# Every fifth weight tile of one phase fetched as 120 and 8 partitions

## The chip, the core and the metric

The kernel runs on one core of a Trainium2 chip. The core has five engines with a queue of instructions each: TensorE (PE, with its weight loads as PEld), VectorE (DVE), ScalarE (ACT), GpSimd (POOL) and SyncE (SP). Transfers between main memory and the on-chip memory, whose rows are 128 partitions, run on 16 DMA engines, whichever queue asks for them. The metric is the device time of one execution, in microseconds.

## What is computed

Two transformer blocks over 256 tokens of width 1024, in 32-bit floats. The first block (two attentions, gates, a mixture of 32 experts) and the even layer of the second lie before the change. The phase around the change is the second block's two PEER layers, with the odd layer's short-convolution mixer between them:

```python
def short_conv_mixer(xn, w_in, conv_w, w_out):
    bg, cg, hx = jnp.split(xn @ w_in, 3, axis=-1)
    u = cg * hx
    y = conv(u, conv_w)            # 3 taps along the tokens, causal
    return (bg * y) @ w_out

def peer(xn, w_q, sub_keys, u, v):
    q = (t @ w_q).reshape(n_tok, 8, 2, 128)
    # two top-16 lists per head, top 16 of their sums: eidx; softmax: gate
    hid = gelu(einsum('td,thkd->thk', t, u[eidx]), approximate=False)
    return einsum('thk,thkd->td', gate * hid, v[eidx])
```

Each token of each PEER layer picks 8 x 16 rows of two tables of 16,384 rows. A final norm follows.

## The kernel before, in words

The tokens are two chunks of 128, one token per partition. The PEER work is a list of 512 positions, `SLOTS`: layer, chunk, head, and which of the head's 16 picks. For each position GpSimd asks for one gather (`pool_ask`, L2812): 128 rows, one per token, of 8 KB each (the row of u and the row of v side by side), 1 MiB in all, into one of nine row buffers. VectorE multiplies the u half with the tokens and sums (L2714), ScalarE applies gelu and the gate (L2768, L2771) and makes a diagonal matrix of the result (L2777), and TensorE multiplies that with the v half and adds into two banks (L2700). Some positions take the last step on VectorE instead (L2720). GpSimd runs five positions ahead (`AHEAD`), and a gather into a buffer waits until the position that used the buffer before is finished. Each gather raises its buffer's semaphore by 16, and VectorE waits for that.

All other work of the phase is laid beside the positions by a table written out by hand (`beside`): at a position p each engine does its part of what `put` placed there. The odd mixer's input products (`"in"`, TensorE L2407), its output products (`"out"`, L2432), the second layer's queries (`"q"`, L2450) and the choosing of the picks on VectorE (L2566 to L2680) are laid out so.

The weights of these products come as tiles of 128 partitions x 8 KB, 1 MiB. SP loads them in `sync_peer` (L2291) in the order of the table with `load` (L270, its DMA is L275). `rings.next_slot` names the slot; SP waits until TensorE has done with the tile that was there, and issues one DMA which raises the slot's semaphore by 16. There are six ring slots and one more tile in the arena; from the middle of the first chunk on only three slots rotate, and four tiles of the mixer and five of the queries serve both chunks. TensorE waits in `tile` for the value that the semaphore has after the tile of that name. The three kinds are 20, 8 and 11 loads, 39 in all.

Of the kernel before, what the change touches and what calls it, by code (L numbers as in the profile page):

```python
# [96 lines left out]
def build(nc, a, out):  # L97
    ctx = ExitStack()
    with ctx:
# [5 lines left out]
        def signal(name):  # L105
            signals.append(Signal(ctx.enter_context(nc.semaphore(name))))
            return signals[-1]

        def table(missing):
            tables.append(Table(missing))  # L110
            return tables[-1]

        pe, ve, ac, po = signal("s_pe_done"), signal("s_dve_done"), signal("s_act_done"), signal("s_pool_done")
        landed = [signal(f"s_slot_landed{i}") for i in range(NSLOT + NX)]
# [7 lines left out]
        slot_of, spent = table(0), table((pe.sem, 1))  # L122
# [74 lines left out]
        rings = Rings()  # L197
# [72 lines left out]
        def load(e, name, src, place=None):  # L270

            s, before = rings.next_slot(name, place)
            if before is not None:
                e.wait_ge(*spent[before])
            e.dma_start(place_of(s)[:, 0:src.shape[1]], src).then_inc(landed[s].sem, landed[s].up(name, by=16))  # L275

        def place_of(s):

            if s < NSLOT:
                return ring[:, s, :]  # L280
            return kept_tile if s == NSLOT else arena[:, 2048 * (s - NSLOT):2048 * (s - NSLOT + 1)]
# [14 lines left out]
        def load_tiles(e, name, w, at_, c0, n, kn=8):  # L296
            for i, (k, m) in enumerate(parts(n, kn)):
                load(e, (name, c0, k), w[at_ + i])
# [140 lines left out]
        def sp_residual(e, n, w):  # L439
            for c0 in (0, 512):  # L440
                for k in (0, 4):
                    load(e, ("res" + n, c0, k), w[c0 // 256 + k // 4])
# [240 lines left out]
        def causal_part(c, lhsT, rhs_of):  # L683
            return (lhsT, rhs_of(0, (c + 1) * P), (c + 1) * P, cm[:, 0:P] if c == 0 else cm[:, P:384], 1.0)
# [21 lines left out]
        def sp_fill_step(e, c0, half):  # L706
            if c0 >= 5664 and half == 0:
                lo = c0 - 5664
                load(e, ("bias", c0), row(b_gate[lo:lo + 512], 512))
            load(e, ("in", c0, 4 * half), w_in[IN_AT[c0] + half])  # L710
# [24 lines left out]
        for c in range(2):  # L735
            for h in range(8):
                mla_jobs.append(dict(
                    c=c, parts=[causal_part(c, qT[:, h, c * P:(c + 1) * P], lambda lo, hi, h=h: kT[:, h, lo:hi])],
# [6 lines left out]
                    c=c, parts=[(qd[p0:p0 + 64, 4 * g + h // 2, c * P:(c + 1) * P],  # L745
                                 kd[p0:p0 + 64, 4 * g + h // 2, 0:kw], kw,
                                 Bm[:, bo + g * kw:bo + (g + 1) * kw], -8.0 * slope) for g in range(3)],
# [1028 lines left out]
        def join_tile(c, c0, k):  # L1776
            return ("join again", c0, k) if c else ("join", c0, k)
# [403 lines left out]
        w_q, w_odd, w_odd_out = a["c_w_q"], a["c_odd_w_in"], a["c_odd_w_out"]  # L2181
# [21 lines left out]
        KEPT_Q = {3: 4, 4: 5, 5: NSLOT, 6: 3, 7: None}  # L2203

        def odd_tile(c, j, k):
            part = (*OB[c][j], k)
            return ("odd", "both", *part) if part in KEPT else ("odd", c, j, k)

        def q_tile(c, h):
            return ("wq", 1, "both", h) if h in KEPT_Q else ("wq", 1, c, h)  # L2210
        OCOL = {"bg": 0, "cg": 1024, "hx": 2048}
# [6 lines left out]
        def norm_steps(p, n, c):  # L2218
            put(p, "square", n, c)
            put(p + 1, "mean", n, c)  # L2220
            put(p + 2, "normed", n, c)
# [66 lines left out]
        put(2 * SEG + 20, "gain", "fin", "mix1")  # L2288
        norm_steps(3 * SEG + 4, "fin", 0)

        def sync_peer(e):  # L2291
            load(e, ("wq", 0, 2), w_q[0, 2], 0)
            load(e, ("wq", 0, 3), w_q[0, 3], 1)
            load(e, ("wq", 0, 4), w_q[0, 4], 2)
            load(e, join_tile(1, 0, 0), w_e_out[0], 3)
            load(e, ("wq", 0, 5), w_q[0, 5], 4)
            load(e, join_tile(1, 0, 4), w_e_out[1], 5)
            load(e, join_tile(1, 512, 0), w_e_out[2], 3)
            load(e, join_tile(1, 512, 4), w_e_out[3], 5)
            load(e, ("wq", 0, 6), w_q[0, 6], 3)  # L2300
            load(e, ("wq", 0, 7), w_q[0, 7], 5)
            for h in range(2):
                load(e, ("wq again", h), w_q[0, h], 5)
            e.wait_ge(ve.sem, ve.at(("joined", 1, 512)))
            for p in range(LAST):
                for what in beside.get(p, ()):
                    if what[0] == "in" and what[3] % 4 == 0:
                        _, c, j, k = what
                        part, hf = OB[c][j]
                        kept = KEPT.get((part, hf, k))  # L2310
                        if kept is None or c == 0:
                            if kept == NSLOT:
                                rings.narrow(3)
                            load(e, odd_tile(c, j, k), w_odd[(OCOL[part] + 512 * hf) // 256 + k // 4], kept)
                    if what[0] == "out" and what[3] % 4 == 0:
                        _, c, hf, k = what
                        load(e, ("oddout", c, hf, k), w_odd_out[2 * hf + k // 4])
                    if what[0] == "q" and what[3] == 0:
                        _, c, h, _ = what
                        if c == 0 or h not in KEPT_Q:  # L2320
                            load(e, q_tile(c, h), w_q[1, h], KEPT_Q.get(h))

        def pe_score(e, L, h, cs_):
            lo, hi = P * cs_[0], P * (cs_[-1] + 1)
# [518 lines left out]
        def sync(e):  # L2843
            sync_first(e)
            sync_moe(e)
            sync_even(e)
            sync_peer(e)
            e.wait_ge(ve.sem, ve.at(("xn", "fin", 0)))
            g = fetched("out0")
            e.dma_start(out[0, 0:P, :], xn[:, 0, :]).then_inc(g.sem, g.up("all", by=16))  # L2850
            g = fetched("out1")
            for c0 in (0, 512):
                e.wait_ge(ve.sem, ve.at(("xn", "fin", 1, c0)))
                e.dma_start(out[0, P:2 * P, c0:c0 + 512], xn[:, 1, c0:c0 + 512]).then_inc(g.sem, g.up("all", by=16))
            for c in range(2):
                g = fetched(f"out{c}")
                e.wait_ge(g.sem, g.at("all"))
# [142 lines left out]
```

## Time and profile before

| | |
|---|---|
| median of 3 runs | 2153.95 us (2153.48 to 2160.74) |
| the profiled execution | 2157.04 us, span 2155.2 us |
| granted TensorE clock, mean | 0.967 of full speed |
| PE / DVE / ACT / POOL busy | 86% / 60% / 33% / 31% |
| software-made DMA queue (gathers) | 542.37 MB, 61.0% of 16 engines |
| SP's DMA queue (weights) | 227.75 MB, 26.3% |

The profile is one execution. "Idle before" in a group is the time in which an engine had nothing running before such an instruction, with what ended it. The chain is followed back from the last instruction to what released each step. DMA share is the mean busy share of the 16 DMA engines, so that one engine of 16 alone shows as 0.06. Matmul ends are modelled, and a TensorE that is 86% busy is not at its peak. A window is a stretch of time, from the start of the span.

### The profile page before, as it was taken

How to read it: one execution, taken by the hardware profiler on the slowest of the kernel's cores; microseconds unless marked ns; L12 is line 12 of the kernel's file. 1: busy time of each engine (PE TensorE's matmuls, PEld its weight loads, DVE VectorE, ACT ScalarE, POOL GpSimd, SP SyncE). 2: the span in 40 equal slices, each digit the busy share in tenths (PEclk: the TensorE clock that was granted, in tenths of full speed). 3: DMA queues.
4: the chain of work that ended last, by engine and by line, in shares of the span. 5: the costliest groups of instructions: out<-in, count | busy, mean ns of one | idle time of the engine just before them, and what ended most of it. 6: DMA issues, size and time to landing. Idle time of an engine off the chain costs nothing.

```text
span 2155.2 us, 20313 instructions
## 1 busy us (share of the span) xinstructions
PE 1852.7 (86%) x5992; PEld 875.6 (41%) x5992; DVE 1286.8 (60%) x3071; ACT 714.8 (33%) x2002; POOL 658.7 (31%) x593
## 2 busy tenths in 40 slices
PE   9999999998799998999877787777888877888876
PEld 4445555333245444455423333333433433334322
DVE  1343433221032777667587787987777888777764
ACT  1232221111011355344343333433333343444442
POOL 2121001110000344343343353453333444434331
PEclk9999999999999999999999999999999889999998
DMA  7432366999795999999999999999999999999995
GB/s 262 159 122 85 125 269 252 416 418 419 295 382 210 409 420 376 420 421 421 421 422 421 421 421 421 420 413 421 421 421 422 403 408 418 421 421 421 421 421 243
DMA packets 115089, 781.50 MB, mean 363 GB/s; under 512 B 16080, under 2 KB 17792, under 8 KB 21664
## 3 DMA queue, kind: packets, MB, share of 16 engines
q0 software_dynamic: 78928, 542.37, 61.0%
q1 hardware_dynamic: 32544, 227.75, 26.3%
q10 hardware_dynamic: 3504, 10.04, 1.2%
q8 instruction: 50, 0.82, 0.2%
q14 instruction: 63, 0.52, 0.1%
HBM read 782.20 MB, written 10.49 MB: 368 GB/s over the span
## 4 chain that ended last, share of the span: by engine, by line
DMA 39%; DVE 14%; PE 7%; issue 7%; POOL 4%; ACT 1%; POOLq 0%; DVEq 0%; ACTq 0%
DMA arena<-in_c_rows_dram,arena 39%; DVE arena L2714 6%; PE banks L2700 3%; POOL arena L2812 3%; PE banks L1824 2%; DVE x L2720 2%; PE banks L1915 1%; DVE arena L2619 1%; ACT arena L2777 0%; DVE arena L2610 0%; DVE arena L2613 0%; DVE arena L2648 0%; DVE arena L2652 0%; DVE arena L2655 0%; PE banks L2334 0%
## 5 line engine op out<-in xcount | busy, mean ns | idle before, releaser
L2700 PE MATMUL banks<-arena 128*128 128x512 f32 x1784 | 893.9, 632 | 242.2 <-ACT arena L2777 240.0
L2812 POOL DMA_INDIRECT arena<-in_c_rows_dram,arena x512 | 581.3, 1135 | 815.8 <-PE banks L2700 452.6
L2714 DVE CUSTOM_DVE_ANT_0 arena<-arena,xn 128x1024 f32<-128x1024 f32 x512 | 626.5, 1224 | 310.8 <-DMA arena<-in_c_rows_dram,arena 307.8
L2700 PEld LDWEIGHTS banks<-arena 128*128 128x128 f32 x1784 | 324.6, 197 | 709.5 <-ACT arena L2777 432.4
L2768 ACT ACTIVATE small<-small 128x1 f32<-128x1 f32 x512 | 103.4, 202 | 719.3 <-DVE small L2714 718.7
L314 PE MATMUL banks<-ring,hT 128*128 128x512 f32 (+1 forms) x480 | 200.4, 573 | 0.0
L376 ACT COPY arena<-banks 128x512 f32<-128x512 f32 (+4 forms) x218 | 101.0, 493 | 281.9 <-PE banks L360 108.3
L2777 ACT ACTIVATE arena<-ident,small 128x128 f32<-128x128 f32 x446 | 179.1, 401 | 41.8 <-ACT small L2771 1.1
L2771 ACT ACTIVATE small<-small 128x1 f32<-128x1 f32 x512 | 150.8, 294 | 49.3 <-DVE arena L2574 0.4
L402 POOL TENSOR_TENSOR small<-small 128x1 f32<-128x1 f32 (+4 forms) x24 | 33.3, 1389 | 320.8 <-DVE small L398 284.9
L314 PEld LDWEIGHTS banks<-ring,hT 128*128 128x128 f32 x480 | 87.3, 190 | 99.0 <-issue 97.3
L2407 PE MATMUL banks<-ring,hT 128*128 128x512 f32 x176 | 91.4, 614 | 1.0 <-ACT hT L376 1.0
L2720 DVE SCALAR_TENSOR_TENSOR x<-arena,small,x 128x1024 f32<-128x1024 f32 x66 | 84.7, 1284 | 7.5 <-ACT small L2771 0.7
L2450 PEld LDWEIGHTS banks<-hT,ring 128*128 128x128 f32 x448 | 67.3, 197 | 49.3 <-issue 48.0
L381 DVE COPY arena<-banks 128x512 f32<-128x512 f32 (+1 forms) x35 | 23.6, 675 | 94.2 <-PE banks L1269 67.2
L1250 PE MATMUL banks<-arena 128*64 128x512 f32 x280 | 71.7, 596 | 3.2 <-DMA arena<-in_c_experts_dram 3.2
L1362 POOL DMA_INDIRECT y_rows<-arena x16 | 16.0, 997 | 183.0 <-ACT arena L376 99.7
L1327 DVE TENSOR_TENSOR arena<-arena,banks 128x256 f32<-128x256 f32 x16 | 6.7, 421 | 104.0 <-ACT arena L1299 104.0
L2450 PE MATMUL banks<-hT,ring 128*128 128x128 f32 x448 | 67.5, 279 | 0.0
L1824 PE MATMUL banks<-ring,hT 128*128 128x512 f32 x144 | 63.6, 592 | 0.0
L360 PEld LDWEIGHTS banks<-ident,arena 128*128 128x128 f32 (+1 forms) x416 | 47.8, 141 | 33.0 <-issue 29.7
L610 DVE SCALAR_TENSOR_TENSOR arena<-arena,banks 128x128 f32<-128x128 f32 (+1 forms) x64 | 19.8, 350 | 66.0 <-PE banks L554 66.0
(319 smaller groups left out, 1819.4 us busy)
## 6 DMA issues: line engine op xcount, KB each, us to landing
arena<-in_c_experts_dram SPq DMA_DIRECT2D x51, 1024.0 KB, 21.4
ring<-in_c_w_in_dram SPq DMA_DIRECT2D x30, 1024.0 KB, 4.8
ring<-in_c_experts_dram SPq DMA_DIRECT2D x30, 1024.0 KB, 26.8
ring<-in_c_odd_w_in_dram SPq DMA_DIRECT2D x19, 1024.0 KB, 9.4
ring<-in_c_w_q_dram SPq DMA_DIRECT2D x18, 1024.0 KB, 9.1
ring<-in_c_even_w_in_dram SPq DMA_DIRECT2D x12, 1024.0 KB, 19.7
arena<-in_c_even_w_in_dram SPq DMA_DIRECT2D x10, 1024.0 KB, 12.4
arena<-in_c_rows_dram,arena POOLq DMA_INDIRECT x512, 17.7
```

The source lines that it names most:

```text
L314: r = e.matmul(banks[:, b, 0:n], lhs[:, k + i, c * P:(c + 1) * P], wt[:, i, :], start=(k + i == 0), stop=(k + i == kn - 1))
L376: e.copy(dst, src).then_inc(ac.sem, ac.up(name))
L1824: r = e.matmul(banks[:, bank_of[name], :], hT[:, k + i, c * P:(c + 1) * P], wt[:, i, :], start=(k + i == 0), stop=(k + i == 7))
L2407: r = e.matmul(banks[:, bank_of[name], :], hT[:, k, c * P:(c + 1) * P], wt[:, k % 4, :], start=(k == 0), stop=(k == 7))
L2450: r = e.matmul(banks[:, bank_of[name], f * P:(f + 1) * P], wt[:, k, f * P:(f + 1) * P], hT[:, k, c * P:(c + 1) * P], start=(k == 0), stop= ...
L2700: r = e.matmul(banks[:, bank_of[("acc", L, c, hf)], :], diag[:, diag_of[m], :], rows[:, row_of[m], D + hf * 512:D + (hf + 1) * 512], start ...
L2714: e.tensor_tensor_reduce(u, u, xn[:, c, :], 1.0, 0.0, ALU.mult, ALU.add, hid3[:, c, h, k:k + 1]).then_inc(ve.sem, ve.up(("u", p)))
L2720: e.scalar_tensor_tensor(x[:, c, :], rows[:, row_of[p - 1], D:2 * D], hid3[:, c, h, k:k + 1], x[:, c, :], ALU.mult, ALU.add).then_inc(ve.s ...
L2768: e.activation(hv, hv, ACT.Gelu).then_inc(ac.sem, ac.up(("gelu", p)))
L2771: e.activation(hv, hv, ACT.Copy, scale=top3[:, c, h, k:k + 1]).then_inc(ac.sem, ac.up(("w", p)))
L2777: e.activation(diag[:, diag_of[p], :], ident[:, :], ACT.Copy, scale=hv).then_inc(ac.sem, ac.up(("diag", p)))
L2812: e.indirect_dma_start(rows[:, b, :], None, table_uv, bass.IndirectOffsetOnAxis(ap=eix[:, c, 16 * h + k:16 * h + k + 1], axis=0)).then_inc ...
```

## The change

A second form of `load`, `load_shared`, takes the same slot, waits the same wait, and issues two DMAs in place of one: partitions 0 to 119 and partitions 120 to 127 of the same tile. Each raises the slot's semaphore by 16, and the name of the tile is bound to the value after both. A counter that starts at zero with `sync_peer` picks the form: of the loads of the odd input products, the odd output products and the second layer's queries every fifth goes by `load_shared`. The other loads of `sync_peer`, and all loads of the stages before, stay as they were, as do slots, waits, the order of issue and what the engines compute.

```diff
+        def load_shared(e, name, src, place=None):
+
+            s, before = rings.next_slot(name, place)
+            if before is not None:
+                e.wait_ge(*spent[before])
+            n = src.shape[1]
+            e.dma_start(place_of(s)[0:120, 0:n], src[0:120, :]).then_inc(landed[s].sem, landed[s].up(by=16))
+            e.dma_start(place_of(s)[120:128, 0:n], src[120:128, :]).then_inc(landed[s].sem, landed[s].up(name, by=16))
...
+        loads = [0]
+
+        def load_row_phase(e, name, src, place=None):
+            loads[0] += 1
+            (load_shared if loads[0] % 5 == 0 else load)(e, name, src, place)
+
         def sync_peer(e):
+            loads[0] = 0
...
-                            load(e, odd_tile(c, j, k), w_odd[(OCOL[part] + 512 * hf) // 256 + k // 4], kept)
+                            load_row_phase(e, odd_tile(c, j, k), w_odd[(OCOL[part] + 512 * hf) // 256 + k // 4], kept)
...
-                        load(e, ("oddout", c, hf, k), w_odd_out[2 * hf + k // 4])
+                        load_row_phase(e, ("oddout", c, hf, k), w_odd_out[2 * hf + k // 4])
...
-                            load(e, q_tile(c, h), w_q[1, h], KEPT_Q.get(h))
+                            load_row_phase(e, q_tile(c, h), w_q[1, h], KEPT_Q.get(h))
```

## Rows read from the trace of the kernel before

**Rows 1.** Page, its 40 slices of 54 us: DMA share and rate.

```profile
span 2155.2 us, 20313 instructions
...
DMA  7432366999795999999999999999999999999995
GB/s 262 159 122 85 125 269 252 416 418 419 295 382 210 409 420 376 420 421 421 421 422 421 421 421 421 420 413 421 421 421 422 403 408 418 421 421 421 421 421 243
```

**Rows 2.** Page, the chain that ended last: by engine, then by line.

```profile
DMA 39%; DVE 14%; PE 7%; issue 7%; POOL 4%; ACT 1%; POOLq 0%; DVEq 0%; ACTq 0%
DMA arena<-in_c_rows_dram,arena 39%; DVE arena L2714 6%; PE banks L2700 3%; POOL arena L2812 3%; PE banks L1824 2%; DVE x L2720 2%; PE banks L1915 1%; DVE arena L2619 1%; ACT arena L2777 0%; DVE arena L2610 0%; DVE arena L2613 0%; DVE arena
```

**Rows 3.** Page, groups: line, engine, op, shapes, count, busy, mean, idle before.

```profile
L2700 PE MATMUL banks<-arena 128*128 128x512 f32 x1784 | 893.9, 632 | 242.2 <-ACT arena L2777 240.0
L2812 POOL DMA_INDIRECT arena<-in_c_rows_dram,arena x512 | 581.3, 1135 | 815.8 <-PE banks L2700 452.6
L2714 DVE CUSTOM_DVE_ANT_0 arena<-arena,xn 128x1024 f32<-128x1024 f32 x512 | 626.5, 1224 | 310.8 <-DMA arena<-in_c_rows_dram,arena 307.8
```

**Rows 4.** Last gathers in GpSimd's timeline; the gather line between 2050 and 2110.

```profile
2120.48 0.95 POOL L2812 DMA_INDIRECT arena<-in_c_rows_dram,arena  x1 [1.53 <-PE banks L2700]
2122.97 0.95 POOL L2812 DMA_INDIRECT arena<-in_c_rows_dram,arena  x1 [1.54 <-PE banks L2700]
...
DMA to landing us min/median/max: 17.1/17.7/18.7
```

**Rows 5.** Tail windows: stretch, length, busy times (count), granted clock, DMA share, GB/s.

```profile
core 0: us, PE busy (x) PEld busy (x) DVE busy (x) ACT busy (x) POOL busy (x), PEclk, DMA share, GB/s
2130.00:2132.00 2.00, 1.51 (x4) 0.68 (x4) 1.23 (x2) 0.53 (x3) 0.00 (x0) 1.00 0.37 156
2132.00:2134.00 2.00, 1.52 (x4) 0.49 (x3) 0.86 (x1) 0.87 (x3) 0.00 (x0) 1.00 0.15 57
2134.00:2140.00 6.00, 3.08 (x7) 0.87 (x5) 3.42 (x7) 1.89 (x7) 0.00 (x0) 0.98 0.06 26
```

**Rows 6.** Windows of the row phase, same columns.

```profile
1390.00:1477.00 87.00, 64.13 (x156) 26.81 (x157) 74.19 (x165) 35.22 (x107) 42.77 (x36) 0.92 1.01 415
1477.00:1531.00 54.00, 42.33 (x118) 19.68 (x117) 32.19 (x63) 17.35 (x53) 19.95 (x17) 0.97 1.01 421
1646.00:1720.00 74.00, 62.38 (x207) 33.10 (x208) 55.81 (x121) 25.94 (x81) 34.63 (x28) 0.93 1.00 408
1720.00:1850.00 130.00, 96.71 (x238) 41.71 (x236) 109.46 (x255) 51.42 (x157) 59.75 (x52) 0.91 1.00 415
1850.00:2120.00 270.00, 226.89 (x610) 98.11 (x608) 190.05 (x451) 115.18 (x351) 107.48 (x107) 1.00 1.01 421
```

**Rows 7.** SP's timeline, its first and last loads; SP's waits, 1010 to 1720.

```profile
1019.90 113.72 SPq L275 DMA_DIRECT2D ring<-in_c_odd_w_in_dram  x8
...
1656.62 60.35 SPq L275 DMA_DIRECT2D ring<-in_c_w_q_dram  x4
...
SPq L275 <- PE banks L2407: 455.0, 17, 168.1
SPq L275 <- PE banks L2432: 158.1, 8, 68.3
```

**Rows 8.** The load line, 1050 to 1700; what TensorE awaited before ring reads.

```profile
L275 SPq DMA_DIRECT2D ring<-in_c_odd_w_in_dram x15: 327/328/1146, 1055.3 to 1582.7; - x15
...
DMA to landing us min/median/max: 8.9/9.7/19.0
...
its engine sat idle before it (us, times) until:
  issue: 73.1, 286
  ACT hT L376: 3.6, 3
```

## The prediction

> **What bounds the kernel now.** I read the page first. The slices show that from about 860 us to the end the 16 DMA engines are busy nearly without a break and move 420 GB/s or a little more, with four slices a little lower [rows 1], and the chain that ended last is 39% DMA, all of it the row gathers [rows 2]. The groups agree: VectorE's dot product at L2714 waits 307.8 us for gathers, and SP's weight loads do not appear as a wait of TensorE [rows 3]. So in this phase time is bytes: 421 GB/s over 16 engines is 26.3 GB/s each, and one engine's sixteenth of a 1 MiB transfer (65,536 B, eight rows of 8 KB) takes 65,536 / 26.3e9 = 2.49 us. The cadence confirms it: gathers are asked for every 2.48 us near the end [rows 4].
>
> Next I ask whether all 16 engines finish together. They don't. The last gather is asked for at 2122.97 us [rows 4], and the windows of the tail show the engines dropping out one by one: 156 GB/s over 2130 to 2132, 57 over 2132 to 2134, and then 26 GB/s, a DMA share of 0.06, over the whole stretch 2134 to 2140 [rows 5]. That is one engine of 16 working alone for about 6 us. A gather is only complete when its last sixteenth is there, so VectorE and the end of the program wait for this one engine. The gathers' 17.7 us from issue to landing between 2050 and 2110 [rows 4], seven times 2.49 us, also says that some engine has a long queue. Yet 421 GB/s in that phase says that the other engines don't run dry either [rows 6]. This is the picture that the sum uses: one straggler about 6 us behind the next engine, and the others busy as well.
>
> **What the change does, step by step.** SP issues 39 loads by the three call sites: 12 and 8 for the odd input products, 4 and 4 for the odd output products, 8 and 3 for the queries. Every fifth is split, so seven are (5, 10, ... 35). Counting issues from 1019.90 us on SP's timeline they fall at about 1055, 1160, 1206, 1477, 1531, 1583 and 1646 us [rows 7].
>
> (1) Seven more DMA instructions on SP, one is 0.33 us at the median [rows 8], 2.3 us in all. What is queued behind them on SP is only the next load. SP waits 455.0 and 158.1 us for TensorE to free slots [rows 7], so it is never late: nothing.
>
> (2) The tile is usable when both parts have landed, which can be one more 8 KB row later, 8,192 / 26.3e9 = 0.31 us, plus the 0.33 us of issue. TensorE shows no wait at all for these tiles, only "issue" and hT [rows 8], and their landing has a median of 9.7 us after issue while the slots are filled some tiles ahead. Nothing. If that cover were gone it would be 7 x 0.64 = 4.5 us at most.
>
> (3) Who carries the bytes. No row of before has a transfer of 120 or 8 partitions, so this is an assumption: a transfer is cut into equal shares over as many of the 16 engines as divide it evenly, 120 over 15 engines with eight rows each and 8 over eight engines with one row each, counted from the first engine. Then the sixteenth engine is spared eight rows, 2.49 us, in each split tile: 7 x 2.49 = 17.4 us. Eight of the others carry nine rows for eight: 7 x 0.31 = 2.2 us more. Seven engines see no change. The Trainium skill, "DMA: Bandwidth & Descriptors", in its section on why a DMA increments its semaphore by 16, has the rule that the largest number up to 16 which divides the slowest dimension is taken, lowest-numbered engines first; by it the shares are these.
>
> (4) Is the spared engine the straggler? The rows name no engine. I take it that it is, as the likeliest case, because the lag is persistent and belongs to one engine [rows 5]. The same page, section "Latency and other measured facts", says that engines 7 and 15 are usually slower than the rest. The trace shows one clear straggler and a second engine leaving last but one, which agrees; by that rule the straggler is spared or, if it is engine 7, loaded further.
>
> (5) What is late next. The straggler's 17.4 us is not the gain: behind it waits the second engine, which finishes at about 2134, 6 us earlier (57 GB/s is two engines' worth, 26 is one [rows 5]; I use 5.6, since the second engine's last bytes may still be landing when the window begins). That engine is also busy without a gap, so its end cannot move forward. If it is one of the first eight it ends 2.2 us later than now. So the gain lies between 5.6 - 2.2 = 3.4 us and 5.6 us. I take 3.4, because eight of the fifteen candidates carry the extra row. By the page's rule the second engine would be number 7, which is one of the eight.
>
> (6) The cost of the odd shapes themselves. In the stretch 1477 to 1531, with five loads in it, the rate is 421 GB/s, as in 1850 to 2120 with none [rows 6], so mixing loads and gathers costs nothing beyond bytes. The odd shape could still hit the wrong write ports. Lower bound zero; it can't be below zero beyond what is counted in (3), since the bytes are the same. Upper bound: each split tile takes every engine as long as two, 2.49 us more, 17.4 us in all. The nearest row, the mixed stretch, is at zero, and I take zero. The same page's "Rules for kernel authors" speaks against the change: two transfers to disjoint partitions serialize, use one of 128. By it the change brings nothing, which is rival (c) below, 2154.0; no run here shows it yet.
>
> Sum: the profiled execution took 2157.04 us with a span of 2155.2; less 3.4 that is 2153.6. The median of the three runs shown is 2153.95, 3.1 below the profiled one, and I forecast against it: 2153.95 - 3.4 = **2150.5 us**.
>
> **The rivals.**
> (a) The straggler is one of the eight that get the extra row. Nothing in the rows excludes it. Then the end moves 2.2 us back: 2156.1 us.
> (b) Slower, by port collisions: the shares of the 120-partition transfer don't line up with the partitions that each engine writes in a gather, two engines meet at one place, and all engines lose time while a split tile is in flight. For it: the rate is at the same ceiling in every full stretch, so there is no slack. Against: each place gets the same bytes in the end. It beats the gain from 3.4 / 7 = 0.5 us per split tile. At half the upper bound, 1.25 us, it is 8.7 - 3.4 = 5.3 us slower, 2159.3; it passes the 0.5% mark only from 2.0 us per tile.
> (c) No effect: the two parts are spread otherwise, or the straggler's lag doesn't come from how many bytes it is given, and it is soon as late as before. 2154.0.
> (d) Bigger gain: since rows come complete earlier, GpSimd asks for the next ones earlier and the short dips are filled. They are 415 GB/s over 87 us, 408 over 74 and 415 over 130 [rows 6], so (6 x 87 + 13 x 74 + 6 x 130) / 421 = 5.4 us of idle. 5.6 + 5.4 = 11.0, 2143.0. Against: the second engine doesn't seem to idle in them.
> (e) The 120 partitions go over eight engines, 15 rows each, and the 8 over the same: 16 rows for 8 on each of them, 2.49 us more per tile, 17.4 in all. If the straggler is not among them, 17.4 - 5.6 = 11.8 later, 2165.8; if it is, 2171.4.
>
> **How the numbers follow.** Forecast 0.44; (a) 0.15; (b) 0.16; (c) 0.10; (d) 0.08; (e) 0.07. About 0.5%, 10.8 us, is what a measurement of this kernel can tell from no change. The forecast, (a), (c) and most of (b) and (d) lie inside. Faster by more needs (d) at its full size: 0.04. Slower by more needs (e) or the upper end of (b): 0.10. Within: 0.86. The range leaves out (e) and the ends of (b) and (d): 2145 to 2163 us.
>
> **What would show it.** Right: the tail's stretch at 26 GB/s shrinks from about 6 us to under 5 and ends some 3 us earlier, the last gathers land some 14 us after their issue where it is now 17.7, the median landing of gathers falls, and the full stretches stay at 421 GB/s. (a) shows as a tail as long as now or longer. (b) shows as less than 421 GB/s in the stretches with split tiles, 1055 to 1720. (e) shows as eight engines alone at some 210 GB/s and the 128-row tiles landing late. The forecast is wrong if the tail shrinks and the time does not, since then the second engine, or VectorE, had more slack or less than I read.

## The result

The median went from 2156.68 us (2153.48 to 2160.74, four runs) to **2192.11 us** (2189.34 to 2193.26, four runs). The ratio is 1.016, with a 95% interval of 1.0148 to 1.0172: 35.4 us slower, 5.1 us for each of the seven split tiles. I had forecast 2150.5, and a range up to 2163. The forecast was set against 2153.95, the median of three of the four runs of before. Ratios here compare executions in the usual, fast state alone; one of e1's nine, 2527.22 us at a granted clock of 0.70, is left out of its ratio.

First the page of the kernel after: its slices, the queues (packets, MB, share of 16 engines' span), the chain and the three groups that answer to [rows 1 to 3].

```profile
span 2191.5 us, 20320 instructions
DMA  7432276999695999999999999999999999999995
GB/s 251 163 120 96 111 294 250 416 418 419 268 407 198 422 421 370 421 422 420 389 421 389 386 421 417 421 419 376 389 387 387 399 421 416 410 421 421 421 420 245
...
q0 software_dynamic: 78928, 542.37, 60.9%
q1 hardware_dynamic: 32593, 227.75, 26.5%
...
DMA 39%; DVE 14%; issue 8%; PE 6%; POOL 4%; ACT 1%; POOLq 0%; DVEq 0%; ACTq 0%
...
L2716 PE MATMUL banks<-arena 128*128 128x512 f32 x1784 | 902.0, 637 | 267.7 <-ACT arena L2793 265.8
L2828 POOL DMA_INDIRECT arena<-in_c_rows_dram,arena x512 | 581.0, 1135 | 850.9 <-PE banks L2716 466.7
L2730 DVE CUSTOM_DVE_ANT_0 arena<-arena,xn 128x1024 f32<-128x1024 f32 x512 | 626.0, 1223 | 344.5 <-DMA arena<-in_c_rows_dram,arena 341.4
```

The DMA digits say nothing: nine tenths in every slice of the row phase, as before. The GB/s below them do. Eight slices at 376 to 399 stand where before had 421, in one of them 403 [rows 1]. Busy engines move less. VectorE's dot product (L2730 is L2714 of before, L2716 is L2700, L2828 is L2812) does the same 626 us of work and waits 341.4 us for gathers in place of 307.8 [rows 3]: 33.6 us of the 36.3 by which the span grew.

**Where it went.** The same 750 us of both kernels in 40 slices of 18.75 us, from the DMA view between 1010 and 1760. Before:

```profile
GB/s 422 420 422 421 422 422 419 422 421 422 420 422 421 421 420 422 422 421 422 419 402 414 422 423 419 421 421 422 419 423 420 421 422 421 422 420 367 424 422 420
DMA packets 43224, 314.38 MB, mean 419 GB/s; under 512 B 4799, under 2 KB 4799, under 8 KB 4927
```

After:

```profile
GB/s 422 421 395 351 422 421 422 420 367 381 421 349 392 419 421 422 421 419 411 421 423 421 419 419 420 398 308 423 421 329 419 423 322 420 421 377 364 420 357 424
DMA packets 41407, 300.89 MB, mean 401 GB/s; under 512 B 4628, under 2 KB 4628, under 8 KB 4756
```

The issues of the 120-partition part (L283) on SP's timeline of after:

```profile
1059.45 0.41 SPq L283 DMA_DIRECT2D ring<-in_c_odd_w_in_dram  x1
1168.69 0.35 SPq L283 DMA_DIRECT2D ring<-in_c_odd_w_in_dram  x1
1219.03 0.45 SPq L283 DMA_DIRECT2D ring<-in_c_odd_w_out_dram  x1
1494.70 0.35 SPq L283 DMA_DIRECT2D ring<-in_c_w_q_dram  x1
1554.54 0.35 SPq L283 DMA_DIRECT2D ring<-in_c_odd_w_in_dram  x1
1609.51 0.35 SPq L283 DMA_DIRECT2D ring<-in_c_odd_w_in_dram  x1
1676.78 0.35 SPq L283 DMA_DIRECT2D ring<-in_c_odd_w_out_dram  x1
```

Seven issues and seven dips, each in the slice of its issue or the one behind it, and mostly about 421 between them. The dip of before at slice 37 (367) is another one and stands in after at slice 39 (357). The seven dips of after lack 96, 94, 101, 136, 92, 99 and 101 GB/s against 421 (each the sum over its one or two slices), 719 in all, times 18.75 / 421 = 32.0 us. The means say the same: (419 - 401) x 750 / 421 = 32.1 us. So nearly the whole loss lies right behind the split tiles.

**Whose packets slowed.** Part 3 of before's page:

```profile
q0 software_dynamic: 78928, 542.37, 61.0%
q1 hardware_dynamic: 32544, 227.75, 26.3%
```

q0 carries the gathers, q1 SP's loads. A share times the span is the time of an engine: q1 went from 0.263 x 2155.2 = 566.8 to 0.265 x 2191.5 = 580.7 us, q0 from 1314.7 to 1334.6 us, with the same bytes. That is 14 us more in the loads and 20 us more in the gathers, though nothing of the gathers was changed (each share is rounded, so either figure is good to 2 us). Per tile that is 2.0 and 2.8 us, each good to 0.3.

**What a reader of gathers sees.** VectorE's timeline of before behind the fifth load, which is still whole there:

```profile
1058.82 1.23 DVE L2714 CUSTOM_DVE_ANT_0 arena<-arena,xn 128x1024 f32<-128x1024 f32 x1 [1.87 <-DMA arena<-in_c_rows_dram,arena]
1063.48 1.23 DVE L2714 CUSTOM_DVE_ANT_0 arena<-arena,xn 128x1024 f32<-128x1024 f32 x1 [3.42 <-DMA arena<-in_c_rows_dram,arena]
1068.44 1.22 DVE L2714 CUSTOM_DVE_ANT_0 arena<-arena,xn 128x1024 f32<-128x1024 f32 x1 [2.55 <-DMA arena<-in_c_rows_dram,arena]
```

The same three positions of after, where that load is the first split one:

```profile
1062.94 1.23 DVE L2730 CUSTOM_DVE_ANT_0 arena<-arena,xn 128x1024 f32<-128x1024 f32 x1 [2.18 <-DMA arena<-in_c_rows_dram,arena]
1070.53 1.22 DVE L2730 CUSTOM_DVE_ANT_0 arena<-arena,xn 128x1024 f32<-128x1024 f32 x1 [6.36 <-DMA arena<-in_c_rows_dram,arena]
1076.50 1.23 DVE L2730 CUSTOM_DVE_ANT_0 arena<-arena,xn 128x1024 f32<-128x1024 f32 x1 [3.56 <-DMA arena<-in_c_rows_dram,arena]
```

VectorE gets its gathers 7.6 and 6.0 us apart here, where it was 4.7 and 5.0. The profile writes the wait to the gather; what differs from before is the form of the load.

The windows over the two stretches, columns as in [rows 5], the last two DMA share and GB/s; first before, then after:

```profile
1058.00:1073.00 15.00, 12.55 (x24) 5.43 (x24) 7.36 (x21) 3.81 (x14) 4.00 (x4) 0.78 1.01 419
1062.00:1077.00 15.00, 9.61 (x20) 3.82 (x20) 3.98 (x10) 2.30 (x8) 2.84 (x4) 0.79 1.02 303
```

(421 - 303) x 15 / 421 = 4.2 us lost here, with the DMA engines busy throughout (1.02).

**The tail**, windows of after with the columns of [rows 5]:

```profile
2166.00:2168.00 2.00, 1.51 (x4) 0.49 (x3) 0.84 (x1) 0.84 (x3) 0.00 (x0) 1.00 0.38 160
2168.00:2170.00 2.00, 1.50 (x4) 0.49 (x3) 0.78 (x3) 0.90 (x3) 0.00 (x0) 1.00 0.12 49
2170.00:2176.00 6.00, 3.53 (x8) 1.06 (x6) 3.42 (x7) 1.59 (x6) 0.00 (x0) 1.00 0.07 29
```

The landing of its gathers issued between 2050 and 2150:

```profile
DMA to landing us min/median/max: 16.1/17.7/18.7
```

One engine still works alone for 6 us, and gathers still take 17.7 us. The relief on which the forecast was built isn't there.

### The profile page after: what moved, and what is told of

Its sections match the earlier page's. It is cut to its first block, busy times and chain, and to the rows that moved or that the text cites. A ratio compares the mean times of both kernels' runs of the same rounds, so it can differ in the third digit from the quotient of the medians.

```text
span 2191.5 us, 20320 instructions
## 1 busy us (share of the span) xinstructions
PE 1864.3 (85%) x5992; PEld 879.5 (40%) x5992; DVE 1287.0 (59%) x3071; ACT 715.3 (33%) x2002; POOL 658.4 (30%) x593
## 3 DMA queue, kind: packets, MB, share of 16 engines
q1 hardware_dynamic: 32593, 227.75, 26.5%
## 4 chain that ended last, share of the span: by engine, by line
DMA 39%; DVE 14%; issue 8%; PE 6%; POOL 4%; ACT 1%; POOLq 0%; DVEq 0%; ACTq 0%
DMA arena<-in_c_rows_dram,arena 39%; DVE arena L2730 7%; POOL arena L2828 4%; PE banks L1833 2%; PE banks L2716 2%; DVE x L2736 2%; PE banks L2350 1%; PE banks L1924 1%; DVE arena L2635 1%; DVE arena L2626 1%; DVE arena L2629 1%; DVE arena L2664 0%; DVE arena L2668 0%; DVE arena L2671 0%; PE banks L369 0%
## 5 line engine op out<-in xcount | busy, mean ns | idle before, releaser
L2716 PE MATMUL banks<-arena 128*128 128x512 f32 x1784 | 902.0, 637 | 267.7 <-ACT arena L2793 265.8
L2828 POOL DMA_INDIRECT arena<-in_c_rows_dram,arena x512 | 581.0, 1135 | 850.9 <-PE banks L2716 466.7
L2730 DVE CUSTOM_DVE_ANT_0 arena<-arena,xn 128x1024 f32<-128x1024 f32 x512 | 626.0, 1223 | 344.5 <-DMA arena<-in_c_rows_dram,arena 341.4
L2716 PEld LDWEIGHTS banks<-arena 128*128 128x128 f32 x1784 | 326.2, 198 | 738.7 <-ACT arena L2793 458.6
## 6 DMA issues: line engine op xcount, KB each, us to landing
arena<-in_c_rows_dram,arena POOLq DMA_INDIRECT x512, 17.7
```

The costliest lines, as they stand in the source:

```text
L2716: r = e.matmul(banks[:, bank_of[("acc", L, c, hf)], :], diag[:, diag_of[m], :], rows[:, row_of[m], D + hf * 512:D + (hf + 1) * 512], start ...
L2730: e.tensor_tensor_reduce(u, u, xn[:, c, :], 1.0, 0.0, ALU.mult, ALU.add, hid3[:, c, h, k:k + 1]).then_inc(ve.sem, ve.up(("u", p)))
L2828: e.indirect_dma_start(rows[:, b, :], None, table_uv, bass.IndirectOffsetOnAxis(ap=eix[:, c, 16 * h + k:16 * h + k + 1], axis=0)).then_inc ...
```

## The experiments

The first theory, *places*, supposes this: in the 128-partition transfers each DMA engine writes certain partitions; a transfer of another size deals its rows out anew, so an engine writes where another is writing its gather rows, and both go slower. The rivals: *count* (fifteen engines, or engines with unequal shares, work badly), *small* (the transfer of 8 partitions is slow in itself), *two* (two transfers for a tile). Unless said otherwise an edit replaces the two transfers of `load_shared` by what is shown, for the same seven tiles. e3, e6 and e8 to e11 leave parts of these tiles unloaded, so they compute with old weights there and serve for their times alone.

Two readings recur. One is the window of 15 us that starts some 3 us behind the issue of the first such tile, as shown above for before (419 GB/s) and after (303).

The other is q1's number of packets. A 128-partition tile is 128 rows of 8 KB. If every engine that takes part adds one packet (its signal), a whole tile is 144, and a split one is 120 + 15 + 8 + 8 = 151. After has 32,593 - 32,544 = 49 = 7 x 7 more. e3 and e6 give the parts one by one: 32,481 is 63 = 7 x 9 fewer (120 + 15 = 135), 31,648 is 896 = 7 x 128 fewer (8 + 8 = 16). So fifteen and eight engines took part, as step (3) had it.

### e1: halves by columns

```
e.dma_start(place_of(s)[:, 0:n // 2], src[:, 0:n // 2]).then_inc(landed[s].sem, landed[s].up(by=16))
e.dma_start(place_of(s)[:, n // 2:n], src[:, n // 2:n]).then_inc(landed[s].sem, landed[s].up(name, by=16))
```

> The same seven tiles in two transfers, but cut by columns: 128 partitions x 4 KB twice. Theories of the 35 us: (places) the 120-partition transfer gives each DMA engine other partitions than it writes in a gather, so that two engines meet at the same partitions' entry and all slow down; (count) a transfer over 15 engines is slow in itself; (small) the 8-partition transfer, 64 KB into eight neighbouring partitions, is the slow one; (two) two transfers for one tile cost this whatever their shape. Places, count and small expect 2157 us as before, within 4. Two expects about 2192.

Measured: 2156.74 us beside 2156.44 of the kernel before, ratio 1.0006 (0.9994 to 1.0019). Its window behind the first such tile:

```profile
1057.00:1072.00 15.00, 9.48 (x24) 3.65 (x22) 7.87 (x22) 3.92 (x13) 5.58 (x5) 1.00 1.02 418
```

418 GB/s, hardly a dip. *Two* falls: twice the transfers, over the same partitions, cost nothing.

### e2: halves by partitions

```
e.dma_start(place_of(s)[0:64, 0:n], src[0:64, :]).then_inc(landed[s].sem, landed[s].up(by=16))
e.dma_start(place_of(s)[64:128, 0:n], src[64:128, :]).then_inc(landed[s].sem, landed[s].up(name, by=16))
```

> The same seven tiles as 64 and 64 partitions, each over all 16 engines with four rows each. Places expects it slow, 4 to 7 us for each of the seven tiles, 2185 to 2205 us, because each half occupies only half of the partitions. Count and small expect 2157, since both parts go over 16 engines and neither is small. Two expects 2192. The rate in the stretches with a split tile tells too: under 400 GB/s by places, 421 by count and small.

Measured: 2183.42, ratio 1.0117 (1.0096 to 1.0138), 27.0 us or 3.9 per tile. Its window:

```profile
1058.00:1073.00 15.00, 10.64 (x20) 4.67 (x20) 5.05 (x13) 2.67 (x10) 4.71 (x4) 0.80 1.01 321
```

The dip is there, 321 GB/s. As many bytes and transfers as e1, no small transfer, sixteen engines for each (112 = 7 x 16 packets more than before, the 16 being a second transfer's signals). Neither *count* nor *small* can be the main cause.

### e3: the 120 partitions alone

```
e.dma_start(place_of(s)[0:120, 0:n], src[0:120, :]).then_inc(landed[s].sem, landed[s].up(name, by=16))
```

> The seven tiles get only their first 120 partitions; the last 8 partitions of those tiles are left out, so 64 KB less for each and old weights in them. Places and count expect the whole loss to stay, 7 x 5.1 us, 2187 to 2195. Small and two expect 2157 or a little under it. If part of the loss goes with the small transfer the time lies between.

Measured: 2181.13, ratio 1.0108 (1.0088 to 1.0129). The bytes left out are worth 7 x 65,536 / 421e9 = 1.1 us, so the large part costs 24.7 + 1.1 = 25.8 us, 3.7 per tile. That is less than expected: the rest of the 5.1, some 1.4 us, goes with the small part. Its window behind the first tile:

```profile
1059.00:1074.00 15.00, 10.35 (x20) 4.35 (x19) 5.25 (x14) 2.65 (x9) 3.96 (x4) 0.82 1.02 323
```

And its tail:

```profile
2158.00:2164.00 6.00, 3.55 (x8) 1.06 (x6) 3.41 (x7) 1.57 (x6) 0.00 (x0) 1.00 0.08 31
```

Seven times 2.49 us spared on one engine with nothing given to the others, and one engine still ends 6 us late.

### e4: 112 and 16

```
e.dma_start(place_of(s)[0:112, 0:n], src[0:112, :]).then_inc(landed[s].sem, landed[s].up(by=16))
e.dma_start(place_of(s)[112:128, 0:n], src[112:128, :]).then_inc(landed[s].sem, landed[s].up(name, by=16))
```

> The same seven tiles as 112 and 16 partitions, seven rows and one row on each of 16 engines, so every engine carries exactly the same bytes as before. Count expects 2157. Places expects it slow, since seven rows per engine can't be the partitions that the engine writes in a gather, 2175 to 2200 us. Small expects a loss smaller than that of the change, since 128 KB go to sixteen neighbouring partitions, 2157 to 2175. Two expects 2192.

Measured: 2180.12, ratio 1.0103 (1.008 to 1.0125), 23.7 us or 3.4 per tile. Its window:

```profile
1062.00:1077.00 15.00, 9.41 (x21) 3.87 (x21) 5.67 (x15) 3.07 (x10) 4.27 (x4) 0.89 1.01 344
```

Sixteen engines again (112 packets more), by equal shares seven rows and one row on each: every engine has exactly the bytes that it has in the kernel before. Besides the second transfer, which cost nothing in e1, what differs is only where it writes them and in what order.

### e5: every tenth tile

```
(load_shared if loads[0] % 10 == 0 else load)(e, name, src, place)
```

> The change as it is, but for every tenth load: three tiles are split in place of seven. If the loss is a price per split tile, 35.4 / 7 = 5.1 us, the time is 2156.5 + 15.2 = 2171.7, between 2168 and 2175. If the loss were a shift of the schedule that sets in with the first split, it stays above 2180; if it grows only where two losses overlap, it falls under 2165.

Measured: 2173.38 beside 2155.67, ratio 1.008 (1.0063 to 1.0097): 17.7 us for three tiles, 5.9 each (4.5 to 7.0 by the interval, which holds the 5.1). The loss grows with the number of split tiles; it isn't paid once.

### e6: the last 8 partitions alone

```
e.dma_start(place_of(s)[120:128, 0:n], src[120:128, :]).then_inc(landed[s].sem, landed[s].up(name, by=16))
```

> The seven tiles get only their last 8 partitions, the other 120 are left out: 960 KB less for each, 2.33 us at 421 GB/s, 16.3 us less in all. Without any price of the shape 2140. The runs so far give the 8-partition part 35.7 - 24.7 = 11 us on top of the 120-partition part, 1.6 us each. If this price is its own (64 KB from eight engines into eight neighbouring partitions) the time is 2140 + 11 = 2151; if it only comes from meeting the 120-partition transfer, 2140 to 2143.

Measured: 2147.95, ratio 0.9956 (0.994 to 0.9972). The 120 partitions left out are 7 x 983,040 / 421e9 = 16.3 us, so 2139.4 was due if the small transfer cost its bytes alone. The 8.6 us above that are 1.2 per transfer of 64 KB (0.7 to 1.7 by the interval), nearer to the price of its own than to none. Its window shows the smaller dip, 389 GB/s:

```profile
1059.00:1074.00 15.00, 11.96 (x25) 4.87 (x26) 7.91 (x22) 4.31 (x15) 5.23 (x5) 0.89 1.01 389
```

With e3's 3.7 it makes 4.9 of after's 5.1: within the noise, the two parts' prices add up.

### e7: the same split where no gathers run

In the first stage, before any gather, all 34 tiles of 2048 columns are loaded in two parts. The row phase is that of the kernel before.

```
if first_stage[0] and n == 2048:
    e.dma_start(place_of(s)[0:120, 0:n], src[0:120, :]).then_inc(landed[s].sem, landed[s].up(by=16))
    e.dma_start(place_of(s)[120:128, 0:n], src[120:128, :]).then_inc(landed[s].sem, landed[s].up(name, by=16))
```

> The kernel before, with all 1 MiB loads of the first stage (the first block's projections, before any row gather runs) cut into 120 and 8 partitions, and none of the row phase. There a 1 MiB load has the DMA engines nearly to itself and lands after a median of 4.8 us. Places: the 120-partition transfer is slow by itself, because eight engines pairs meet, so its landing rises to 6.5 to 8 us. If the loss needs the gathers beside it, the landing stays at 4.8 to 5.3 us. The row phase stays at 421 GB/s and the total moves by what the first stage loses.

Measured: 2160.03, ratio 1.002 (1.001 to 1.0031). The profile has no landing for such a pair, since both raise one semaphore, so I read the windows instead. The kernel before:

```profile
100.00:200.00 100.00, 99.58 (x335) 50.08 (x334) 39.72 (x93) 31.67 (x82) 16.25 (x3) 1.00 0.31 111
200.00:300.00 100.00, 97.62 (x490) 54.62 (x489) 38.79 (x98) 31.68 (x65) 0.00 (x0) 1.00 0.33 127
```

The same stretches of e7:

```profile
100.00:200.00 100.00, 99.58 (x333) 49.85 (x332) 36.69 (x89) 31.99 (x83) 16.25 (x3) 1.00 0.51 117
200.00:300.00 100.00, 97.62 (x471) 54.10 (x470) 40.38 (x101) 32.69 (x68) 0.00 (x0) 1.00 0.53 125
```

No row gather is in flight in these stretches. The loads' queue on the page of e7:

```profile
q1 hardware_dynamic: 32782, 227.75, 29.5%
```

For the same bytes the engines are busy 1.6 times as long: 111 / 0.31 = 358 GB/s while busy, then 117 / 0.51 = 229. Over the whole run q1 takes 0.295 x 2157.0 = 636 us in place of 567, 69 us for 34 tiles (238 = 34 x 7 more packets), **2.0 us per tile**: what after's loads lost too. An engine's own share of 2.49 us takes nearly twice as long, and no gather is needed for that. TensorE, 99.58 us busy of 100 in both, bounds this stage, so the loss is hidden but for 4.4 us. The theory in its first form, that loads meet gathers, is too narrow: split loads are slow among themselves. Whether the rows of one transfer, its two parts or two tiles in a row get in each other's way this run doesn't tell.

### e8, e9: 64 partitions, at two places

One transfer of 64 partitions in place of the tile, in e8 and below it in e9:

```
e.dma_start(place_of(s)[0:64, 0:n], src[0:64, :]).then_inc(landed[s].sem, landed[s].up(name, by=16))
```
```
e.dma_start(place_of(s)[32:96, 0:n], src[32:96, :]).then_inc(landed[s].sem, landed[s].up(name, by=16))
```

> The seven tiles get only partitions 0 to 63, the other half is left out: 512 KB less for each, 8.7 us less in all, so 2147 without any price of the shape. Places, made exact: an engine writes a gather's rows to two groups of four partitions, the first eight engines 4e and 32 + 4e, the last eight 64 above these. Four consecutive rows per engine over 0 to 63 then put engines e and e + 8 into the same engine's place, two to a place, and the eight places above 64 stay empty. It expects the transfer at half rate, 1.9 us lost for each, 2147 + 13 = 2160, between 2155 and 2164. If any transfer of 64 partitions were as good as another, this one and the next give the same time.

> The same with partitions 32 to 95 in place of 0 to 63: the same bytes, the same 64 partitions, the same 16 engines with four rows each. By the exact form of places every engine now writes rows of its own place and no two meet: no loss, 2147, between 2143 and 2150, and the stretches with a cut tile at 421 GB/s. Any theory that goes by size, count or shape alone expects the same time as for partitions 0 to 63.

Measured: e8 2161.59, ratio 1.0026 (1.0012 to 1.0039); e9 2146.99, ratio 0.9959 (0.9945 to 0.9974), both beside 2155.75. The bytes left out are 8.7 us. e9 gains 8.8, its bytes and nothing else; e8 loses 5.8 where it should gain 8.7. Number of transfers, bytes, shape, packets (32,096 in both) and engines are the same; 14.6 us, 2.1 per transfer, come with the place alone (which rows of the tile are read goes with it). The window of e8:

```profile
1056.00:1071.00 15.00, 11.90 (x23) 5.34 (x24) 6.87 (x17) 3.25 (x11) 3.96 (x4) 0.80 1.01 366
```

And that of e9:

```profile
1061.00:1076.00 15.00, 12.17 (x27) 5.42 (x28) 8.14 (x23) 3.96 (x13) 5.66 (x5) 0.90 1.02 421
```

The same 750 us as above in 40 slices, e8:

```profile
GB/s 423 421 378 421 421 422 420 421 374 421 404 388 422 422 421 421 422 420 421 420 402 412 396 426 420 369 420 423 375 421 395 398 420 422 374 421 398 426 419 422
```

And e9:

```profile
GB/s 422 421 420 422 421 422 420 421 423 421 419 423 421 421 421 422 420 423 420 421 423 419 416 421 417 421 421 420 421 421 422 421 421 420 421 405 399 424 419 423
```

e8 has a dip at each of its seven tiles (378, 374, 404 and 388, 369, 375, 395 and 398, 374), e9 none; its 405 and 399 are the dip that before has at 367.

This pair decides against size, count and shape, and for *places* as a matter of which partitions are covered. The Trainium skill, "DMA: Bandwidth & Descriptors", section "The descriptor swizzle", says that in a 128-partition transfer an engine writes two groups of four partitions 32 apart, engines 0 to 7 below partition 64 and 8 to 15 above it, and "SBUF — State Buffer", section "Door 1: The DMA port swizzle", that these eight partitions hang on one port. If rows are dealt out in order, four to an engine, 0:64 puts two engines on each of eight ports, and 32:96 puts every engine on a port of its own: the two runs agree. The Trainium skill says too, in "SBUF — State Buffer", section "Can I just issue two DMAs to hit both halves?", that the only way to reach all 16 ports is one transfer over all 128 partitions; e9's 421 GB/s speaks against that.

### e10, e11: 60 partitions over fifteen engines, 40 over ten

Both at a place where, dealt out in order, each engine has its own.

```
e.dma_start(place_of(s)[32:92, 0:n], src[32:92, :]).then_inc(landed[s].sem, landed[s].up(name, by=16))
```
```
e.dma_start(place_of(s)[32:72, 0:n], src[32:72, :]).then_inc(landed[s].sem, landed[s].up(name, by=16))
```

> Partitions 32 to 91: 60 partitions, so 15 engines with four rows each, every one in its own place by the same map, and one engine without a row. Places expects no loss: 544 KB less for each tile, 9.3 us less in all, 2146.5. Count (15 engines are slow in themselves) expects it as slow as the 120-partition transfer or half of that, 2158 to 2171. The spared engine is relieved by 17.4 us against the kernel before; if it were the one that works alone at the end, the tail's stretch with one engine would be gone.

> Partitions 32 to 71 of the seven tiles, the other 88 left out: four rows on each of ten engines, in their own places, and six engines without a row, 17.4 us less for these six and 8.7 us less for the ten. It asks which group holds the engine that works alone at the end. If it is one of the six spared ones, it is no longer alone: the tail's stretch of about 6 us at one engine's rate is gone and the time is set by the next engine, some 2 to 6 us under the 2147 of the run with 64 partitions. If it is one of the ten, the time stays at 2147, within 3, and the stretch stays about 6 us.

Measured: e10 2148.05 beside 2155.75, ratio 0.9959 (0.9941 to 0.9977), 7.7 us less for bytes worth 9.3; e11 2146.36 beside 2158.37, ratio 0.995 (0.9933 to 0.9966), 12.0 us less (7.3 to 14.5 by the interval) for bytes worth 12.0. Their windows behind the first tile show 421 and 420 GB/s. Packets are 483 = 7 x 69 fewer in e10 (60 + 15 for 144) and 658 = 7 x 94 in e11 (40 + 10), so fifteen and ten engines took part. So *count* falls for fifteen engines too. That an uneven load of the engines costs nothing fits, but isn't sharp: 8.7 us less is due if the engines that carry four rows for eight set the time, and both intervals hold it. The tail of e10:

```profile
2129.00:2135.00 6.00, 2.92 (x7) 0.79 (x5) 3.42 (x7) 2.02 (x8) 0.00 (x0) 1.00 0.07 31
```

That of e11:

```profile
2124.00:2130.00 6.00, 3.03 (x7) 0.87 (x5) 3.42 (x7) 1.90 (x8) 0.00 (x0) 1.00 0.07 31
```

The lone engine's 6 us are there whether one engine or six carry nothing of seven tiles. Either the straggler is among the ten that carry their rows in every variant, or its lag is not made by how many bytes it was given and is back within the 450 us behind the last such tile. The time of e11 doesn't settle it: less its own kernel before it lies 3.2 us under e9, which is within the noise. No run tells these two apart, and none names the engine.

## Why the prediction was wrong

**Steps (1) and (2)**, issue and landing: held. Of SP's waits in after (engine and line, released by; us, times, longest) the largest is at the first part of a split tile itself:

```profile
SPq L283 <- PE banks L2423: 254.5, 4, 167.9
```

So the extra issues were free. TensorE's idle time before ring reads in after, and the landing of whole tiles between 1050 and 1700:

```profile
  issue: 74.5, 286
  ACT hT L385: 3.6, 3
...
DMA to landing us min/median/max: 9.1/14.8/18.5
```

There is no wait for a load, as before [rows 8]. This though whole tiles now land later: the median was 9.7. The cover of some tiles ahead held that too.

**Step (3)**, the shares: the number of engines held, as the packets show. Which engines they are, no row says.

**Step (4)**, the spared engine is the straggler: failed as far as the runs tell. After, e3, e10 and e11 spare the engines beyond the fifteenth or tenth, and the tail stays at 6 us. From "one engine is always last" I went to "it is the one that this change spares", though the rows named none; they gave it one chance in sixteen. The Trainium skill's "DMA: Bandwidth & Descriptors", section "Latency and other measured facts", on which I leaned, names engines 7 and 15; if shares start from the lowest engine, 15 is the one spared here, and its relief shows nowhere. Of 7 these runs say nothing.

**Step (5)**, the second engine as the limit of the gain: never came to bear. Its 3.4 us were taken from 2153.95; from the four-run median they would have given 2153.3.

**Step (6)** is the one that cost 35 us, the price of the odd shapes. I took zero from the mixed stretch at 421 GB/s [rows 6]. But all transfers of that stretch, loads and gathers, had 128 partitions. It showed that loads and gathers share the engines for nothing, and nothing about a transfer whose rows are dealt out otherwise. That was the unknown, and the nearest row didn't contain it. The upper bound failed too. "Each split tile takes every engine as long as two" is the tile's own 2.49 us; it left out that gathers in flight beside it slow as well. The packets of loads took 2.0 us per tile more, those of gathers 2.8, and the time says 5.1: about 2 x 2.49, where the bound was one.

**The rivals.** (b), collisions at one place, is the one that the runs bear out. I named it, gave it 0.16 and priced it at half of a bound that was itself half of the truth: 1.25 us per tile where 5.1 was measured. Its argument against, that each place gets the same bytes in the end, is true and beside the point: e4 keeps each engine's bytes and 0:128 is filled in all cases, and it costs 3.4 us per tile all the same. That two engines at one place take turns there, so that places go unused meanwhile, is the theory's account and no row shows it. Its sign, less than 421 GB/s behind the split tiles between 1055 and 1720, is what the trace shows seven times. The trace of (e), eight engines alone at 210 GB/s, does not appear. The rule that step (6) cites from the Trainium skill, "DMA: Bandwidth & Descriptors", section "Rules for kernel authors", says that two transfers to disjoint partition halves serialize; I took it for 120 and 8 as well, and by it the time would have stayed at 2154.0. e2 shows that even such halves cost 3.9 us per tile more than the whole tile, and e1 that a pair over all partitions costs nothing.

**Shown and argued.** Shown: the loss is per split tile, falls on loads and gathers, arises on the loads' queue without gathers too, adds up from the two parts within the noise, and is decided by which rows of the tile a transfer covers, with bytes, shape, packets and number of engines equal (e8 against e9). Argued: that the contested thing is the port of a group of partitions of the on-chip memory, and that rows are dealt out in order. Both fit all eleven runs and foretold e8's and e9's times to 2 us, but no row here shows which engine wrote which partition. Two rivals stand untested. All three fast partial transfers (e9, e10, e11) start at partition 32, and no slow one does, so a rule that goes by the start alone isn't excluded. And every edit moves the rows read in main memory along with the partitions written, so a cause on the reading side isn't either; e1, which reads all rows in two pieces at no cost, doesn't test it.

## What to carry to other kernels

Where DMA is the bound, read GB/s and not the busy digits: here the engines counted as busy at 303 GB/s (1.02) as at 421. Keep large loads over all 128 partitions, and cut a tile by columns if it has to be cut: that cost nothing here, while the three cuts by partitions (120 and 8, 64 and 64, 112 and 16) cost 3.4 to 5.1 us a tile, and a part of that falls on what is in flight beside it. And when a row is to price something that the trace doesn't hold, ask whether the row contains the one property that is new; if it doesn't, the range has to stay open on the bad side.

## What the hardware showed that I had not expected

A transfer of 64 partitions runs at full rate or not by where it starts: 32:96 moved with the gathers at 421 GB/s, 0:64 with 366 over the 15 us behind it. The split tiles slowed the gathers' queue by more (2.8 us a tile) than their own (2.0 us). A load of 8 partitions, 64 KB, costs 1.2 us beyond its bytes beside a full stream, and these are worth 0.16. And one engine works alone for 6 us at the end also where the sixteenth, or the last six, had been spared.
